# A two-block model kernel: modulation sums re-ordered, head, seams and tail by halves and token tiles

## The chip, the cores and the metric
The kernel runs on one core of a Trainium2 chip. The metric is the device time of one execution in microseconds (us). PE is TensorE (matmuls), PEld its weight loads, DVE VectorE, ACT ScalarE, POOL GpSimd, SP SyncE, whose queue issues most transfers.

## What is computed
One token sequence of 256 tokens and width 2048 goes through two models in fp32. The first block is a norm, an input product (attention of 8 heads and a convolution branch), an output product, a gated residual, and a feed-forward layer of width 8192. The second block has two layers, each with a modulated norm:

```python
shift, scale, gate = m[..., :D_MODEL], m[..., D_MODEL:2 * D_MODEL], m[..., 2 * D_MODEL:]   # m = silu(c) @ mod_w + b
h = _rmsnorm(x, pre_g) * (1 + scale) + shift
proj = h @ w_in
...                                   # even layer: attention over x and ctx; odd layer: pooling
x = x + gate * _rmsnorm(y @ w_out, post_g)
```

The even layer (`ev_`) also modulates a context (`shift_c`, `scale_c`), the odd layer (`od_`) doesn't.

## The kernel before
Every large product is cut into blocks of 512 output columns, each with 8 steps of 256 rows of the weight. A step's weight (128 x 1024 elements on chip) comes by SP's queue into `raw`, 1 MB for two steps. ACT rounds it to `w_hi` (`split_hi`, L530), DVE subtracts to get `w_lo` (`split_lo`, L1053), and PE multiplies activations (`hi`, `lo`) with both. Four slots of `w_hi` and `w_lo` let the splits run four steps ahead: the split of a step can start when PE is through with the step four before it. Blocks follow in this order: `u` (4), `qkv` (6), `out` (4), `ff` (32: four groups of four hidden and four outer blocks), `evq` (4), `evkv` (2, each step double, over x and ctx), `evz` (4, between the attention heads), `evo` (4), `odu` (4), `odg` (4), `pool`, `odo` (4).

Each engine runs its own list of instructions in the written order, and semaphores join them. DVE's list is written by hand: `run_ahead(b, between)` (and `most_ahead`, `each_ahead`) puts two splits and then whatever `between(m)` holds, four times per block: splits (4, 5) and (6, 7) of block b, then (0, 1) and (2, 3) of the next.

In these places stand the modulation sums. Each modulation vector (6 units, L71) is a sum over 16 tiles of 128 rows; each tile comes as two halves of 512 KB into `mod_raw[:, half]` by POOL's queue (`load_half`, L458; `first_loads`, L465), and each half is one multiply-add of 128 x 1024 by DVE into `mod_sum` (`mod_step`, L1080). A unit of two vectors has two such operations per half. POOL issues the load for half n when half n - 2, which used the same buffer, is summed. `each(unit, h0, counts)` (L1103) deals halves out to the four places of a block. When a unit is complete, `mod_turn` turns it by four DVE operations (two block transposes, two reduces), `sum_mod` (L1914) adds the partitions on PE, and `mod_out` writes the columns.

A seam stands between `out` and `ff`, `ff` and `evq`, `evo` and `odu`: ACT squares the last output block of each of the two token tiles, DVE multiplies with the gain (`gained`, `ff_gained`), `post_scale` makes the residual's scale, `gained_products` and `residual_sums` get the next norm without reading the residual again, `add_to_residual` updates X, and `transposes` on PE (L1894, or L1892 at the first) feeds `norm_product`. At the head the same transposes wait for x, the constants and the first norm. At the tail `post_scale` and `add_to_residual` are followed by four output transfers of 512 KB from SP.

POOL's list also copies queries for the second model's heads (`stage_q`), and `head_slots` on POOL puts one load of a modulation half behind each copy.

Of the kernel before, what the change touches and what calls it, by code (L numbers as in the profile page):

```python
# [70 lines left out]
MOD_UNITS = [("ev_gate", 1), ("od_shift", 1), ("ev_shift", 2), ("ev_scale", 2), ("od_scale", 1), ("od_gate", 1)]  # L71
# [30 lines left out]
def build_program(nc, io, out):  # L102
# [6 lines left out]
    with ExitStack() as ctx:  # L109
# [142 lines left out]
        x_first = [sem(f"x_first{i}") for i in range(TT)]  # L252
# [70 lines left out]
        mod_scales = sem("mod_scales")  # L323
# [19 lines left out]
        def _(sp):  # L343
# [24 lines left out]
            sp.dma_start(quad[:], io["quad"]).then_inc(const_in, 16)  # L368
            sp.dma_start(qk_gain[:, 0, :], io["q_norm"].partition_broadcast(P)).then_inc(const_in, 16)
            sp.dma_start(qk_gain[:, 1, :], io["k_norm"].partition_broadcast(P)).then_inc(const_in, 16)  # L370
            sp.dma_start(table[:, 0:512], io["dist_neg"]).then_inc(table_in, 16)

            W = weights["w_in"]
            with sp.Fori(0, 2) as i:
                for par, c0 in ((0, 4096), (1, 3072)):
                    load_block(BLOCK["u"] + 2 * i + par, W, rows(), bass.ds(c0 + BW * i, BW))
# [70 lines left out]
            for n in range(2 * TT):  # L447
                tt, half = n % TT, slice(D // 2 * (n // TT), D // 2 * (n // TT + 1))
                sp.wait_ge(h_ready, 24 + 4 * (n // TT) + TT + tt + 1)
                sp.dma_start(out[tt * P:(tt + 1) * P, half], X[:, tt, half]).then_inc(out_done, 16)  # L450
            sp.wait_ge(out_done, 16 * 2 * TT)
# [3 lines left out]
        def _(pool):  # L455
# [38 lines left out]
            first_loads("od_scale", "od", 1, "ev_scale")  # L494
            load_mod("od_scale", "od", 1, 1, KT // 2 - 1)
# [6 lines left out]
            def head_slots(i, slots, loads=True):  # L502
                for j in slots:
# [4 lines left out]
                    if loads:  # L508
                        load_half("od_scale", "od", 1, KT // 2 + 1 + 2 * i + j // 2, j % 2)
# [531 lines left out]
        def _(dve):  # L1041
# [637 lines left out]
            def evo_beside(n):  # L1679
# [3 lines left out]
                def go(m):  # L1683
# [10 lines left out]
                    if n:  # L1694
                        gate(m)
# [555 lines left out]
```

## Time and profile before
| | us |
|---|---|
| median of 3 runs (range) | 1888.36 (1885.23 to 1890.24) |
| profiled execution, own time | 1888.55 |
| its span, first to last instruction | 1886.9 |
| PE busy in the span | 1820.1 (96%) |
| DVE busy | 1457.7 (77%) |
| ACT busy | 900.3 (48%) |
| mean granted clock of PE | 0.990 |
| read from HBM | 421.23 MB |

The page gives shares over the whole span. The stages have different limits, so the places where PE stands still are to be looked up in windows and in the timelines of the engines around them.

### The profile page before, as it was taken

Reading aid. Unit: us, or ns where it says so; the run is one execution under the profiler, and the core shown is the slowest. Engines: PE = TensorE matmul, PEld = TensorE weight load, DVE = VectorE, ACT = ScalarE, POOL = GpSimd, SP = SyncE. Lnnn points to the kernel's source line nnn. Section 1 sums busy time; section 2 is a strip of 40 time slices with the busy share of each in tenths; the row PEclk is TensorE's granted clock in tenths of the full one; section 3 lists DMA queues with packets and bytes.
Section 4 is the critical chain, followed back from the end, with each engine's and each line's share of the span. In section 5 each row is a group of like instructions: output and inputs, shape, how many; then the busy total and the mean of one; then the engine's idle time right before and its main releaser. Section 6 shows DMA issues by size and latency. Waiting matters only on the chain.

```text
span 1886.9 us, 26488 instructions
## 1 busy us (share of the span) xinstructions
PE 1820.1 (96%) x10068; PEld 1573.7 (83%) x10068; DVE 1457.7 (77%) x1671; ACT 900.3 (48%) x1158; POOL 116.1 (6%) x217
## 2 busy tenths in 40 slices
PE   6999999999999999999999979999999998999997
PEld 6999978788888888888888768888888887888986
DVE  4799996778878898898788987745677677887854
ACT  5343456464434543443344447523556545445452
POOL 0100000100110000000000000000111000000000
PEclk9999999999999999999999989999999999999999
DMA  7865545948998788777977747645544684768662
GB/s 263 291 195 183 159 155 194 331 156 278 325 318 279 240 287 281 234 243 260 266 244 250 262 157 266 200 158 177 168 145 158 242 291 140 252 223 260 209 223 89
DMA packets 189737, 426.94 MB, mean 226 GB/s; under 512 B 12352, under 2 KB 12736, under 8 KB 187840
## 3 DMA queue, kind: packets, MB, share of 16 engines
q1 hardware_dynamic: 161984, 324.80, 50.7%
q0 software_dynamic: 27648, 100.68, 16.3%
q8 instruction: 74, 1.21, 0.3%
q14 instruction: 31, 0.25, 0.0%
HBM read 421.23 MB, written 4.21 MB: 225 GB/s over the span
## 4 chain that ended last, share of the span: by engine, by line
PE 81%; DVE 11%; DMA 4%; ACT 2%; issue 2%; SPq 0%; DVEq 0%; POOLq 0%; ACTq 0%; POOL 0%
PE banks L1831 18%; PE banks L1854 12%; PE banks L1855 12%; PE banks L1856 12%; PE banks L1833 9%; PE banks L1819 4%; PE banks L1820 4%; PE banks L1821 4%; DVE w_lo L1053 3%; DMA mod_raw<-in_ev_mod_w 2%; DVE mod_sum L1242 2%; PE banks L1894 2%; DVE mod_sum L1092 2%; PE banks L2120 1%; PE banks L2136 1%
## 5 line engine op out<-in xcount | busy, mean ns | idle before, releaser
L530 ACT ACTIVATE w_hi<-raw 128x1024 fp32r<-128x1024 f32 x552 | 579.2, 1058 | 697.9 <-PE banks L1856 330.9
L1053 DVE TENSOR_TENSOR w_lo<-raw,w_hi 128x1024 fp32r<-128x1024 f32 x552 | 666.8, 1221 | 233.5 <-ACT w_hi L530 231.4
L1831 PE MATMUL banks<-a_pair,w_hi 128*128 128x512 f32 x1536 | 546.1, 400 | 1.8 <-DVE w_lo L1053 1.5
L1833 PE MATMUL banks<-a_pair,w_lo 128*128 128x256 f32 x1536 | 431.9, 281 | 0.0
L1831 PEld LDWEIGHTS banks<-a_pair,w_hi 128*128 128x128 f32 x1536 | 289.3, 188 | 74.3 <-DVE w_lo L1053 2.2
L1092 DVE SCALAR_TENSOR_TENSOR mod_sum<-mod_raw,silu_c,mod_sum 128x1024 f32<-128x1024 f32 x240 | 301.5, 1280 | 48.0 <-DMA mod_raw<-in_ev_mod_w 24.0
L1854 PE MATMUL banks<-w_hi,b_hi 128*128 128x512 f32 x832 | 326.2, 392 | 4.2 <-DVE w_lo L1053 4.2
L1856 PE MATMUL banks<-w_hi,b_lo 128*128 128x512 f32 x832 | 323.9, 389 | 0.0
L1855 PE MATMUL banks<-w_lo,b_hi 128*128 128x512 f32 x832 | 323.7, 389 | 0.0
L1833 PEld LDWEIGHTS banks<-a_pair,w_lo 128*128 128x128 f32 x1536 | 290.9, 189 | 0.1
L1819 PE MATMUL banks<-a_pair,w_hi 128*128 128x256 f32 x768 | 222.1, 289 | 3.3 <-DVE w_lo L1053 2.9
L1821 PE MATMUL banks<-a_pair,w_lo 128*128 128x256 f32 x768 | 217.9, 284 | 0.0
L1820 PE MATMUL banks<-a_pair,w_hi 128*128 128x256 f32 x768 | 217.9, 284 | 0.0
L1854 PEld LDWEIGHTS banks<-w_hi,b_hi 128*128 128x128 f32 x832 | 156.2, 188 | 39.2 <-issue 7.1
L1856 PEld LDWEIGHTS banks<-w_hi,b_lo 128*128 128x128 f32 x832 | 156.2, 188 | 32.8
L1855 PEld LDWEIGHTS banks<-w_lo,b_hi 128*128 128x128 f32 x832 | 156.2, 188 | 31.9
L1819 PEld LDWEIGHTS banks<-a_pair,w_hi 128*128 128x128 f32 x768 | 148.0, 193 | 4.6 <-DVE w_lo L1053 3.3
L1854 PE MATMUL banks<-w_hi,a_pair 128*128 128x512 f32 x384 | 151.6, 395 | 0.0
L1855 PE MATMUL banks<-w_lo,a_pair 128*128 128x512 f32 x384 | 149.6, 389 | 0.0
L1856 PE MATMUL banks<-w_hi,a_pair 128*128 128x512 f32 x384 | 149.5, 389 | 0.0
L1820 PEld LDWEIGHTS banks<-a_pair,w_hi 128*128 128x128 f32 x768 | 148.1, 193 | 0.1
L1821 PEld LDWEIGHTS banks<-a_pair,w_lo 128*128 128x128 f32 x768 | 147.9, 193 | 0.0
(202 smaller groups left out, 1612.3 us busy)
## 6 DMA issues: line engine op xcount, KB each, us to landing
raw<-in_w_ff SPq DMA_DIRECT2D x128, 1024.0 KB, 6.7
mod_raw<-in_ev_mod_w POOLq DMA_DIRECT2D x96, 512.0 KB, 5.2
mod_raw<-in_od_mod_w POOLq DMA_DIRECT2D x96, 512.0 KB, 5.4
raw<-in_w_in SPq DMA_DIRECT2D x40, 1024.0 KB, 5.1
raw<-in_ev_w_in SPq DMA_DIRECT2D x40, 1024.0 KB, 5.8
raw<-in_od_w_in SPq DMA_DIRECT2D x32, 1024.0 KB, 6.7
raw<-in_w_out SPq DMA_DIRECT2D x16, 1024.0 KB, 5.3
raw<-in_ev_w_out SPq DMA_DIRECT2D x16, 1024.0 KB, 6.9
```

Of the source, the lines that this page charges most:

```text
L530: nc.scalar.activation(w_hi[:, s % SLOTS], raw[:, s // 2, KPS * (s % 2):KPS * (s % 2) + KPS, :], ACT.Copy).then_inc(hi_ready, 1)
L1053: nc.vector.tensor_tensor(w_lo[:, s % SLOTS], raw[:, s // 2, KPS * (s % 2):KPS * (s % 2) + KPS, :], w_hi[:, s % SLOTS].bitcast(F32), ALU.s ...
L1092: nc.vector.scalar_tensor_tensor(s, mod_raw[:, half, :], c, s, ALU.mult, ALU.add).then_inc(mod_acc, 1)
L1242: e = nc.vector.scalar_tensor_tensor(y, src, w, y, ALU.mult, ALU.add)
L1819: nc.tensor.matmul(o, wh, hi[:, k, :], start=first and t == 0 and f % 2 == 0, stop=False, skip_group_check=True)
L1820: nc.tensor.matmul(o, wh, lo[:, k, :], start=False, stop=False, skip_group_check=True)
L1821: last = nc.tensor.matmul(o, wl, hi[:, k, :], start=False, stop=t == KPS - 1, skip_group_check=True)
L1831: nc.tensor.matmul(out[:, f, :], wh, rows[:, :, k, :], start=s == 0 and t == 0, stop=False, skip_group_check=True)
L1833: last = nc.tensor.matmul(out[:, f, T:2 * T], wl, rows[:, 0, k, :], start=False, stop=s == STEPS - 1 and t == KPS - 1, skip_group_check=True)
L1854: nc.tensor.matmul(o, ah, w_hi[:, slot, t, :], start=s == 0 and t == 0, stop=False, skip_group_check=True)
L1855: nc.tensor.matmul(o, ah, w_lo[:, slot, t, :], start=False, stop=False, skip_group_check=True)
L1856: last = nc.tensor.matmul(o, lo[:, k, P * tt:P * (tt + 1)], w_hi[:, slot, t, :], skip_group_check=True, start=False, stop=s == STEPS - 1 a ...
```

## The change
It has these parts.

Head: `ident` is loaded first on a semaphore of its own, x comes in four loads, `cols` behind it, and the other constants behind the first block's weights. ACT squares half a tile and a quarter, DVE squares the last quarter. Norm pairs and weight splits alternate in block one. POOL's first modulation loads wait until four splits are done.

Modulation: the order of units is `ev_gate`, `ev_shift`, `ev_scale`, `od_shift`, `od_scale`, `od_gate`. `od_shift` leaves the `ff` stage and takes the places of `evq` block 2 and `evkv`; `od_scale` takes 24 halves in the heads and 8 in `evo`; `od_gate` has 2 in `evo` and 30 in `odu` and `odg`. `ev_scale`'s turn is at places 228 to 238 of `ff`, its PE sum ahead of the last outer block.

Last steps: in `out`, the last `ff` block, `evo` and `odo`, PE runs steps 6 and 7 of token tile 0 first and then of tile 1, and squares and gain products of tile 0 start at `tile_done`.

Tail: DVE adds five of eight pieces to the residual, ACT and POOL the other three; each piece is its own output transfer.

```diff
-MOD_UNITS = [("ev_gate", 1), ("od_shift", 1), ("ev_shift", 2), ("ev_scale", 2), ("od_scale", 1), ("od_gate", 1)]
+MOD_UNITS = [("ev_gate", 1), ("ev_shift", 2), ("ev_scale", 2), ("od_shift", 1), ("od_scale", 1), ("od_gate", 1)]
+HEAD_HALVES = ((0,), (1, 2), (3,), (4, 5))
+DVE_PIECES = [(0, 0), (1, 0), (0, 1), (1, 1), (0, 2)]
+POOL_PIECES = [(1, 2), (0, 3), (1, 3)]
...
-            for tt in range(TT):
-                sp.dma_start(X[:, tt, :], io["x"][tt * P:(tt + 1) * P, :]).then_inc(x_first[tt], 16)
-            sp.dma_start(ident[:], io["ident"]).then_inc(const_in, 16)
-            sp.dma_start(cols[:], io["cols"]).then_inc(const_in, 16)
+            sp.dma_start(ident[:], io["ident"]).then_inc(ident_in, 16)
+            for n in range(2 * TT):
+                half = slice(D // 2 * (n % 2), D // 2 * (n % 2 + 1))
+                sp.dma_start(X[:, n // 2, half], io["x"][n // 2 * P:(n // 2 + 1) * P, half]).then_inc(x_first[n], 16)
+            sp.dma_start(cols[:], io["cols"]).then_inc(cols_in, 16)
...
+            pool.wait_ge(split_done, 8 + 4)
             first_loads("ev_gate", "ev", 2)
             load_mod("ev_gate", "ev", 2, 1, KT)
-            first_loads("od_shift", "od", 0)
-            load_mod("od_shift", "od", 0, 1, KT)
             first_loads("ev_shift", "ev", 0)
             load_mod("ev_shift", "ev", 0, 1, KT)
             first_loads("ev_scale", "ev", 1)
             load_mod("ev_scale", "ev", 1, 1, KT)
-            first_loads("od_scale", "od", 1, "ev_scale")
-            load_mod("od_scale", "od", 1, 1, KT // 2 - 1)
+            first_loads("od_shift", "od", 0, "ev_scale")
+            load_mod("od_shift", "od", 0, 1, 12)
...
             pool.wait_ge(q_T_ready, 5)
             stage_q(0, 0)
-            load_mod("od_scale", "od", 1, KT // 2 - 1, KT // 2 + 1)
+            load_mod("od_shift", "od", 0, 12, KT)
+            first_loads("od_scale", "od", 1, "od_shift")
             with pool.Fori(0, 3) as i:
                 head_slots(i, range(4))
...
                     else:
-                        halves("od_scale", i, 1)
+                        halves("od_shift", i, 1)
...
-            run_ahead(BLOCK["evkv"], each("od_scale", 4, (1, 2, 1, 2)))
+            run_ahead(BLOCK["evkv"], each("od_shift", 4, (3, 4, 4, 3)))
...
-            run_ahead(BLOCK["evkv"] + 1, each("od_scale", 10, (1, 2, 1, 2)))
+            def last_keys_beside(m):
+                each("od_shift", 18, (4, 4, 4, 2))(m)
+                if m == 3:
+                    mod_turn("od_shift", 0, 0, 3, raw_temp)
+            run_ahead(BLOCK["evkv"] + 1, last_keys_beside)
...
-                    mod_step("od_scale", KT // 2 + 2 * i + j // 2, j % 2)
+                    for c in HEAD_HALVES[j]:
+                        mod_step("od_scale", 3 * i + c // 2, c % 2)
...
+                    if n < 2:
+                        halves("od_scale", 24 + 4 * n + m, 1)
+                    elif n == 2:
+                        turn_parts("od_scale", 0, 1, 3, raw_temp, m, 1)
...
-            gate_steps = [(1, 1, 1, 0)] * 2 + [(1, 0, 1, 0)] * 2 + [(0, 0, 0, 0)] + [(1, 1, 1, 1)] * 2 + [(2, 2, 0, 0)]
+            gate_steps = [(1, 1, 1, 1), (1, 1, 1, 0), (1, 1, 1, 0), (1, 0, 1, 0), (0, 0, 0, 0), (2, 2, 2, 1), (2, 2, 2, 1), (2, 2, 0, 0)]
...
+            def last_steps(steps, a2, hi, lo):
+                for tt in range(TT):
+                    for s, slot in steps:
+                        for t in range(KPS):
...
+                        if tt == TT - 1:
+                            e.then_inc(step_done, 1)
+                    if tt < TT - 1:
+                        e.then_inc(tile_done, 1)
...
-                if n == 1:
-                    sum_mod("od_scale", 1, 3)
+                if n == 2:
+                    sum_mod("od_scale", 2, 3)
```

In each seam the list of DVE changes alike; at `evo` it is:

```diff
-            post_scale(6, lambda: gained_products(NBLK - 1))
+            def last_tile(tt):
+                gained(2 * (2 * NBLK - 1), NBLK - 1, acc[0], gained_tile, [tt])
+                dve.wait_ge(gained_tile, TT * (2 * NBLK - 1) + tt + 1)
+                gained_products(NBLK - 1, [tt])
+            last_tile(0)
+            dve.wait_ge(y_squared, 2 * TT * NBLK)
+            post_scale(6, lambda: last_tile(1))
```

## Rows read from the trace of the kernel before

**Rows 1.** The page, parts 1 and 5: busy shares; VectorE's weight splits.
```profile
PE 1820.1 (96%) x10068; PEld 1573.7 (83%) x10068; DVE 1457.7 (77%) x1671; ACT 900.3 (48%) x1158; POOL 116.1 (6%) x217
...
L1053 DVE TENSOR_TENSOR w_lo<-raw,w_hi 128x1024 fp32r<-128x1024 f32 x552 | 666.8, 1221 | 233.5 <-ACT w_hi L530 231.4
```

**Rows 2.** Timeline, head: start us, us, engine line op, idle before and releaser.
```profile
9.73 1.91 ACT L547 ACTIVATE scratch<-scratch 128x2048 f32<-128x2048 f32 x1 [1.92 <-DMA scratch<-in_x]
...
13.98 0.17 DVE L1212 TENSOR_SCALAR neg_sink<-cols 128x8 f32<-128x8 f32 x1 [13.98 <-DMA qk_gain<-in_k_norm]
...
15.32 6.68 PE L1894 MATMUL banks<-ln_rstd,scratch 128*128 128x128 f32 x32 [15.32 <-DVE ln_rstd L1150]
```

**Rows 3.** Timeline, block one: modulation issues on POOL, and PE's hole.
```profile
62.63 0.53 POOL L461 DMA_DIRECT2D mod_raw<-in_ev_mod_w  x1 [1.56 <-DVE mod_sum L1092]
...
69.78 0.53 POOL L461 DMA_DIRECT2D mod_raw<-in_ev_mod_w  x1 [0.72 <-DVE mod_sum L1092]
...
86.27 0.58 PE L1819 MATMUL banks<-a_pair,w_hi 128*128 128x256 f32 x1 [2.69 <-DVE w_lo L1053]
```

**Rows 4.** Timeline, seam 1 (out to ff).
```profile
376.05 0.60 ACT L736 ACTIVATE scratch<-banks 128x512 bf16<-128x512 f32 x1 [4.38 <-PE banks L1856]
...
380.47 2.82 PE L1892 MATMUL banks<-ident,scratch 128*128 128x128 f32 x12 [4.46 <-DVE scratch L1377]
```

**Rows 5.** Timeline, seam 2 (ff to evq).
```profile
1107.39 1.27 DVE L1528 TENSOR_TENSOR scratch<-scratch,banks 128x512 f32<-128x512 f32 x2
...
1111.57 0.16 DVE L1145 RECIPROCAL resid_s<-norm_s 128x2 f32<-128x2 f32 x1
...
1115.32 6.27 PE L1894 MATMUL banks<-ln_rstd,scratch 128*128 128x128 f32 x32 [7.47 <-DVE ln_rstd L1150]
```

**Rows 6.** Timeline, seam 3 (evo to odu).
```profile
1571.50 5.20 PE L1894 MATMUL banks<-ln_rstd,scratch 128*128 128x128 f32 x32 [7.49 <-DVE ln_rstd L1150]
```

**Rows 7.** Windows: length, busy of PE, PEld, DVE, ACT, POOL, clock, DMA, GB/s.
```profile
4.00:5.00 1.00, 0.00 (x0) 0.00 (x0) 0.00 (x0) 0.00 (x0) 0.00 (x0) 1.00 1.03 426
...
380.50:386.70 6.20, 6.02 (x22) 5.17 (x23) 5.45 (x10) 5.24 (x16) 0.00 (x0) 0.51 0.04 16
...
1036.00:1084.00 48.00, 44.62 (x192) 35.27 (x191) 44.42 (x49) 22.54 (x34) 3.17 (x6) 1.00 0.78 272
```

**Rows 8.** Timeline, odu and odg: a late half, a split of w_hi.
```profile
1613.03 1.28 DVE L1092 SCALAR_TENSOR_TENSOR mod_sum<-mod_raw,silu_c,mod_sum 128x1024 f32<-128x1024 f32 x1 [5.55 <-DMA mod_raw<-in_od_mod_w]
...
1717.95 1.06 ACT L530 ACTIVATE w_hi<-raw 128x1024 fp32r<-128x1024 f32 x1 [1.77 <-PE banks L1833]
```

**Rows 9.** Timeline, tail: residual adds and output transfers.
```profile
1877.78 5.39 DVE L1377 SCALAR_TENSOR_TENSOR scratch<-scratch,resid_s 128x512 f32<-128x512 f32 x8
...
1879.88 3.64 SPq L450 DMA_DIRECT2D out<-scratch  x4
```

**Rows 10.** Timeline, POOL at the first head: an issue and a copy.
```profile
1316.46 0.53 POOL L461 DMA_DIRECT2D mod_raw<-in_od_mod_w  x1 [0.65 <-DVE mod_sum L1092]
...
1317.32 0.62 POOL L507 COPY scratch<-scratch 128x512 f32 x1
```

**Rows 11.** Timeline: end of evo block 2 on ACT; a reduce of a turn.
```profile
1542.29 1.06 ACT L530 ACTIVATE w_hi<-raw 128x1024 fp32r<-128x1024 f32 x1 [1.66 <-PE banks L1856]
...
1762.67 1.22 DVE L1121 TENSOR_REDUCE mod_part<-mod_raw 128x32 f32<-128x1024 f32 x1
```

**Rows 12.** Timeline, evkv and first head: w_hi, first half, the head's maximum.
```profile
1233.17 1.06 ACT L530 ACTIVATE w_hi<-raw 128x1024 fp32r<-128x1024 f32 x1 [4.38 <-PE banks L1856]
...
1235.40 1.28 DVE L1092 SCALAR_TENSOR_TENSOR mod_sum<-mod_raw,silu_c,mod_sum 128x1024 f32<-128x1024 f32 x1
...
1315.74 1.22 DVE L1646 TENSOR_REDUCE soft<-banks 128x2 f32<-128x1024 f32 x1
```

**Rows 13.** mod_raw by tile: landings in 1230:1312 (evkv), in 1330:1470 (heads).
```profile
DMA to landing us min/median/max: 4.7/5.5/6.0
...
DMA to landing us min/median/max: 3.9/4.1/6.1
```

More of the change, by code:

```diff
@@ L446, in _ @@
                 load_block(BLOCK["odo"] + i, W, rows(), bass.ds(BW * i, BW))
[L447 to L451, printed above, removed]
+            for n, (tt, c) in enumerate(DVE_PIECES):
+                part = slice(BW * c, BW * (c + 1))
+                sp.wait_ge(h_ready, 3 * TT * NBLK + n + 1)
+                sp.dma_start(out[tt * P:(tt + 1) * P, part], X[:, tt, part]).then_inc(out_done, 16)
+            sp.wait_ge(out_done, 16 * TT * NBLK)
         @block.gpsimd
@@ L776, in ff_hidden, with gained_squares @@
                     nc.scalar.activation(b_hi[:, 4 * bi:4 * bi + FT, :], relu, ACT.Square).then_inc(hid_hi, 1)
-            def gained_squares(before, i):
-                for tt in range(TT):
+            def gained_squares(before, i, tiles=range(TT)):
+                for tt in tiles:
                     act.wait_ge(gained_tile, TT * (NBLK * before + i) + tt + 1)
@@ L1035, in _ @@
                     split_hi(b + 1, range(4))
-                row_block("odo", n, n % 2)
+                row_block("odo", n, n % 2, range(TT), 4 if n == 3 else 0)
             root(8)
+            act.wait_ge(resid_ready, 1)
+            act.wait_ge(acc_free, 2 + ACC["odo"] + 4)
+            for tt, c in POOL_PIECES:
+                part = slice(BW * c, BW * (c + 1))
+                nc.scalar.activation(Y[:, tt, part], Y[:, tt, part], ACT.Copy, scale=resid_s[:, tt:tt + 1]).then_inc(tail_scaled, 1)
+            for n, (tt, c) in enumerate(POOL_PIECES):
+                part = slice(BW * c, BW * (c + 1))
+                act.wait_ge(tail_ready, n + 1)
+                nc.scalar.dma_start(out[tt * P:(tt + 1) * P, part], X[:, tt, part]).then_inc(out_done, 16)
         @block.vector
@@ L1355, in gained @@
                         e.then_inc(each_tile, 1)
-                if not each_tile:
+                if not each_tile and TT - 1 in tiles:
                     e.then_inc(acc_free, 1)
@@ L1521, in ff_outer, with last_add @@
                     ff_add(g, bi)
-            def last_add(n):
-                block_done(BLOCK["ff"] + 28 + n)
-                for tt in range(TT):
+            def last_add(n, tiles=range(TT)):
+                for tt in tiles:
+                    if n == NBLK - 1 and tt == 0:
+                        dve.wait_ge(tile_done, 2)
+                    else:
+                        block_done(BLOCK["ff"] + 28 + n)
                     part = ff_sum[:, tt, BW * n:BW * (n + 1)]
@@ L1763, in beside @@
                         gate_sum(n - 5)
-                    each("od_gate", 10 + sum(sum(c) for c in gate_steps[:n]), gate_steps[n])(m)
+                    each("od_gate", 2 + sum(sum(c) for c in gate_steps[:n]), gate_steps[n])(m)
                     if n == 7 and m == 2:
@@ L1800, in _ @@
                     dve.wait_ge(grow_in, 64)
-                gained(2 * (2 * NBLK + n), n, acc[n % 2])
-            dve.wait_ge(acc_free, 2 + ACC["odo"] + 4)
-            post_scale(8)
-            add_to_residual()
+                gained(2 * (2 * NBLK + n), n, acc[n % 2], None, range(TT if n < NBLK - 1 else 1))
+            dve.wait_ge(y_squared, 3 * TT * NBLK)
+            post_scale(8, lambda: gained(2 * (3 * NBLK - 1), NBLK - 1, acc[1], None, [1]))
+            dve.sem_inc(resid_ready, 1)
+            for tt, c in DVE_PIECES:
+                part = slice(BW * c, BW * (c + 1))
+                nc.vector.scalar_tensor_tensor(X[:, tt, part], Y[:, tt, part], resid_s[:, tt:tt + 1], X[:, tt, part],
+                                               ALU.mult, ALU.add).then_inc(h_ready, 1)
         @block.tensor
```

285 lines of the change are left out of this document (165 added, 120 removed).

## The prediction

> **What bounds the kernel now.** I read the page's busy shares, then windows of 4 us to find where TensorE (PE) is not full, then the timeline of every engine around each hole. PE is busy for 1820.1 of 1886.9 us [rows 1]: the holes add up to 67 us, and only what shortens or lengthens one, or changes PE's clock, moves the time. They are 15.3 us at the head [rows 2]; 2.7 at 86 [rows 3]; 4.5, 10.1 and 7.5 at the three seams, where a residual sum and a norm stand between two products [rows 4 to 6]; 3.4 in 1036 to 1084 (48.00 less 44.62) [rows 7]; 1.5 near 1613, where VectorE (DVE) waits 5.55 for a modulation load [rows 8]; 12 after the last matmul [rows 9]. DVE is busy 77%, and makes w_lo of each weight step (1.22) in order with all else [rows 1]: whatever it waits for, w_lo waits for too.
>
> **The change, part by part: gains.**
> - Head. DVE's first instruction waits for the last of five constant loads until 13.98; PE starts at 15.32, 1.34 later. The second tile of x was there at 9.73 [rows 2], though 1 MB of modulation weights came beside it. After, ident and x come alone: 2.16 MB at 426 GB/s [rows 7] from about 2.7 us on (first bytes as before) ends at 7.8, landed about 8.1. One 512-column square (0.75 with its read), a reduce (0.3) and the same 1.34 follow: PE at about 10.4. Gain 4.9; bounds 4.2 (x lands 0.7 later) and 5.5. Weights queue behind x and cols alone and are there before the first transposes end; in block one DVE needs 2.1 us per pair and split, PE 3.8 per step with its transposes. The modulation loads start at about 20 us, their first use is at 40: hidden. The hole at 86 stays, as the rounds that make it stay.
> - Seam 1. PE ends at T = 376.0 and goes on at 380.47 [rows 4]. Tile 0's square and product now lie under tile 1's last 12 matmuls (2.7 us), tile 1's product beside the root. What is left from T: square 0.75, reduce and mean 0.4, product 0.65, reciprocal 0.2, two adds 1.4, hand-overs 0.1: T+3.5. Gain 1.0. The two last steps wait for the later one's split; it was ready 1.4 before the earlier one starts, so this adds nothing.
> - Seam 2. PE ends at T = 1104.9, by windows of 1 us. DVE, still turning the scale vectors, comes to the last sum at 1107.39, PE goes on 7.93 later [rows 5]: 10.4. After, the turn is at places 228 to 238 and DVE is free. Tile 0's four operations with hand-overs take 3.0 from T-2.65; then tile 1: sum to T+1.05, square to 1.85, reduce and mean to 2.25, two products to 3.65, and the chain from the reciprocal on as before, 3.75 less a wait of 0.4 [rows 5]: T+7.1. Gain 3.4 (a wait of 0.1 rounded).
> - Seam 3. PE idles 7.49 [rows 6]. After: square 0.75, reduce and mean 0.4, two products 1.5, the same 3.4 behind: T+6.1. Gain 1.4.
> - Hidden layers. od_shift's 32 halves (128x1024) leave them, the two-vector units get 98 places instead of 80, and the turn comes before the last blocks. The 3.4 in 1036 to 1084 come with DVE busy 44.42 of 48 [rows 7]. They go. Gain 3.4, bound below 2.
> - Tail. A square and a product leave the chain, as at seam 1: the first add is 0.9 earlier than 1877.78. Output starts at 1879.88 after three adds of 0.67 [rows 9], now after one: 2.3 earlier; 2 MB then flow at about 400 GB/s if pieces come in time. DVE makes one per 0.67, the queue needs 0.65. No row has an add on GpSimd; its 128x512 copy takes 0.62 [rows 10], so three adds take between 1.9 and, at twice that, 3.8 us, and either way end before the other five pieces are out. Gain 2.3. The Trainium skill, "GPSIMD Engine Reference", section 3.1, measures 4497 ns for a 2048-element add; the estimate from it is 1.1 per piece, and no row here shows it.
>
> Gains: 4.9+1.0+3.4+1.4+3.4+2.3 = 16.4.
>
> **Costs.** A half of a modulation vector is a 512 KB load into one of two buffers, one DVE operation of 1.28, then the next load of that buffer. In block one a buffer's issues are 7.15 apart (62.63, 69.78), so two halves cost 7.1 where PE takes two w_lo in 5.8, and PE runs dry at 86.27 [rows 3].
> - evkv, the largest. 12 halves become 28 (3,4,4,3 and 4,4,4,2 between pairs of splits), with four turn operations behind them (1.22 for a reduce [rows 11], 4.75 in all, bounds 4.5 and 5). PE wants a w_lo per 5.44 (1.06+4.38) [rows 12]. A round is 1.24 (a half behind another) + 0.68 from its end to the issue (0.65 idle and a step of the queue [rows 10]) + the landing: median 5.5 here, where each load meets a 1 MB weight load, 4.1 in the heads, where few do [rows 13]. I take 4.85, near the middle, as of two loads in a place one will meet the weights: round 6.8. I followed it half by half from 1235.4 [rows 12]: a half starts when its buffer has landed and DVE is free, a split 1.1 after PE frees its slot. Splits and halves of the four places of block 0 end at 1235.4/1243.4, 1246.3/1256.9, 1259.3/1270.5, 1272.9/1281.4; head norm and rope take 6.45; block 1: 1290.2/1299.5, 1301.9/1313.0, 1315.4/1326.5, 1328.9/1333.3; the turn 1338.1. The same account with the counts of before gives 1315.8, and DVE came to the first head's maximum at 1315.74 [rows 12]. So it comes 22.3 late. Queued behind it: the maxima, late rope, softmax and the next w_lo. PE stops: its next scores need a query that GpSimd copies only after two loads that wait for this turn, and its transposes need the softmax. Its slack there was nil (it idled 1.4 in four places). Bounds: landing 4.1 gives 14.1, landing 5.2 (the round of block one) 26.2.
> - After such a hole PE comes back at half clock: after seam 1 it was 0.51 over 6.2 us [rows 7]. Half of about 4 us is 2.0 (bounds 0 and 3).
> - evo. PE's sum of the two od vectors stands behind block 2, but the last turn operation stands behind a split whose slot comes free at the block's end T: ACT 1.06 from T [rows 11], split 1.2, reduce 1.2: PE waits 3.5 (bounds 3.3, and 5.2 with the clock lost).
> - odu. Four halves instead of three stand before splits in the place where the third already waits until 1613.03 [rows 8]: 1.2 more.
> - odg. 12 halves become 18 (2,2,2,1 twice, then 2,2). PE takes a w_lo per 2.83 (1.06+1.77) [rows 8], 5.65 for two, against 6.8 for a pair of halves. A split's slack before its PE step is 6.2. By the same account second splits end 5.8 before their step in the first place, 2.6, 0.3 and 0.1 before it in the fifth, eighth and tenth, and 2.6 after it in the last; with the firsts PE loses 4.3. Bounds 0 (landing 4.1) and 7.1 (5.2).
> - Heads: 24 halves instead of 16, 1.3 each in a period of 10.1 where a softmax is ready 4.7 before PE asks: covered; if not, 1.
>
> Costs: 22.3+2.0+3.5+1.2+4.3 = 33.3; net +16.9 on the profiled execution's 1888.55 (span 1886.9 and 1.65 around it), which is 0.2 from the median of the runs shown, 1888.36. Forecast 1905.
>
> **Rivals.**
> 1. Loads come round faster, and the kernel is not slower. At a landing of 3.2 the account gives 6.3 for evkv and 0 for odg: costs 13.0 against 16.4, 1885. It decides from a landing below about 3.6. For it: evkv has light traffic, and od_shift's loads mostly run alone. Against: the shortest landing of the rows is 3.9 [rows 13]. The Trainium skill, "DMA: Bandwidth & Descriptors", section "Anatomy of one DMA", has 2.0 us plus bytes by 436 GB/s, an estimate of 3.2 for 512 KB; by it this rival is the outcome, and the trace's 4.1 and 5.5 speak against it. Chance 0.13.
> 2. DVE's lateness isn't PE's, as I have a queue's order wrong; 3.5+1.2 remain: 1877. Against: the waits stand in the program order of DVE and GpSimd. Chance 0.07.
> 3. All landings near 4.1: costs 14.1+2.0+3.5+1.2 = 20.8, 1893. Chance 0.15.
> 4. The token tiles bring nothing (tile 0's operations hold DVE when tile 1 is ready, or PE's wait for both splits eats it): gains less 5.8, 1911. Chance 0.1.
> 5. The forecast, landings 4.5 to 5.5: 0.55, 1898 to 1914.
>
> **How the numbers follow.** Low end: rival 3 and a seam 1 whose clock holds (-3), 1889. High end: landing 5.2 and clocks lost, 1888.5-16.4+26.2+3+5.2+1.2+7.1 = 1915, with half of rival 4's loss 1919. A measurement tells 0.3%, 5.7 us, from no change, so "same" is 1882.7 to 1894. Faster: rival 2 and part of rival 1, 0.12. Same: the rest of rival 1 and half of rival 3, 0.15. Slower 0.73.
>
> **What would show it.** PE's first matmul near 10.4; seam holes of 3.5, 7.1 and 6.1; none in 1036 to 1084; a hole of some 20 at the first head, with many DVE waits on od modulation loads before it; one of 3.5 behind evo block 2; several of 1 to 1.5 in odg. I am wrong if evkv's landings are near 3.5, or if PE goes on while DVE lags.

## The result, and the profile after

| | before | after |
|---|---|---|
| median of the runs, us | 1887.09 (4 runs, 1885.23 to 1890.24) | 1921.59 (4 runs, 1918.45 to 1926.26) |
| ratio | | 1.0183, 95% interval 1.0156 to 1.021 |
| profiled span, us | 1886.9 | 1921.2 |
| TensorE (PE) busy, us | 1820.1 | 1829.4 |
| VectorE (DVE) busy, us | 1457.7 | 1462.4 |

The change costs 34 us; 17 were forecast, and 1921.6 lies 2.6 above the top of the range. The first view to read is the page's busy shares with the modulation line, of the kernel after; it answers [rows 1].

```profile
PE 1829.4 (95%) x10068; PEld 1581.5 (82%) x10068; DVE 1462.4 (76%) x1673; ACT 903.6 (47%) x1165; POOL 121.3 (6%) x220
...
L1127 DVE SCALAR_TENSOR_TENSOR mod_sum<-mod_raw,silu_c,mod_sum 128x1024 f32<-128x1024 f32 x240 | 301.1, 1280 | 88.9 <-DMA mod_raw<-in_od_mod_w 65.5
```

PE is idle 25 us more (1921.2 less 1829.4 is 91.8; it was 66.8) and busy 9 us longer for the same 10068 matmuls, which is time at the lower clock. The modulation operations waited 88.9 us in all, 65.5 of it for od loads. The waits of PE, kernel after (line waited for, us in total, times, longest):

```profile
PE banks L1981 <- DVE ln_rstd L1185: 24.7, 3, 12.0
PE banks L2234 <- POOL scratch L507: 20.8, 1, 20.8
PE banks L1897 <- DVE w_lo L1088: 5.7, 5, 2.9
PE banks L1885 <- DVE w_lo L1088: 5.4, 4, 3.2
PE banks L2010 <- issue: 3.6, 1, 3.6
...
PE banks L1885 <- DVE scratch L1815: 3.4, 1, 3.4
PE banks L1979 <- DVE scratch L1414: 3.3, 1, 3.3
PE banks L2169 <- DVE scratch L1628: 3.0, 1, 3.0
```

L1981 is the head (12.0, was 15.3) with seams 2 and 3; L1979 is seam 1 (3.3, was 4.5 in [rows 4]). L2234 is the first head, L2169 the key transposes in evkv, L2010 the sum in evo, L1897 the small holes of odu and odg, and the L1885 that waits for scratch the one before the pooling product. The L1885 that waits for w_lo is mostly block one (3.6 of its 5.4; the 3.2 is the hole that was 2.69 in [rows 3]). The hole at the first head is made by a timeline of DVE like this one (evkv's second block):

```profile
1281.04 2.47 DVE L1127 SCALAR_TENSOR_TENSOR mod_sum<-mod_raw,silu_c,mod_sum 128x1024 f32<-128x1024 f32 x2
1287.66 2.52 DVE L1127 SCALAR_TENSOR_TENSOR mod_sum<-mod_raw,silu_c,mod_sum 128x1024 f32<-128x1024 f32 x2 [4.15 <-DMA mod_raw<-in_od_mod_w]
1290.11 2.75 DVE L1088 TENSOR_TENSOR w_lo<-raw,w_hi 128x1024 fp32r<-128x1024 f32 x2
...
1317.45 2.35 DVE L1088 TENSOR_TENSOR w_lo<-raw,w_hi 128x1024 fp32r<-128x1024 f32 x2
...
1328.26 1.22 DVE L1156 TENSOR_REDUCE mod_part<-mod_raw 128x32 f32<-128x1024 f32 x1
1329.40 1.22 DVE L1696 TENSOR_REDUCE soft<-banks 128x2 f32<-128x1024 f32 x1
```

One sees two halves, 4.15 us of nothing, two halves, and only then the next two w_lo. The first head's maximum comes at 1329.40. PE had ended its last product before that and waited from 1311.

Where the 34 us are. Windows of 2 us over both traces give PE's idle time, and, as busy time multiplied by (1 less the granted clock), at most what the lower clock cost:

| stretch of the trace, us | idle, after less before | clock, after less before | the steps of the prediction there |
|---|---|---|---|
| head (first matmul 11.98, was 15.32) | -3.3 | | -4.9 |
| 14 to 372, without the head | +0.8 | +3.1 | 0 |
| 372 to 392, seam 1 | -1.1 | -1.3 | -1.0 |
| 392 to 1084, hidden layers | -3.4 | 0 | -3.4 |
| 1084 to 1120, seam 2 | -3.4 | -0.7 | -3.4 |
| 1120 to 1350, evkv and first head | +23.3 | +1.7 | +24.3 |
| 1350 to 1540, other heads | 0 | 0 | 0 |
| 1540 to 1600, evo and seam 3 | +2.1 | +4.0 | +2.1 |
| 1600 to 1740, odu and odg | +1.3 | +1.7 | +1.2 |
| 1740 to 1860, rest of odg, pool | +6.2 | +3.3 | +4.3 |
| tail (last matmul to end 14.7, was 12.0) | +2.7 | | -2.3 |

The sum is 36.9 for 34.3 in the spans. Most of the difference lies between seams 1 and 2: PE goes on behind seam 2 at 1103.78, 11.5 earlier than the 1115.32 of [rows 5], where the rows down to there give 8.7. Neither column shows what the rest is.

### The profile page after: what moved, and what is told of

Same layout as the page of the kernel before. It is cut to its first block and busy times, and to the rows that moved or that the text cites. A ratio compares the mean times of both kernels' runs of the same rounds, so it can differ in the third digit from the quotient of the medians.

```text
span 1921.2 us, 26445 instructions
## 1 busy us (share of the span) xinstructions
PE 1829.4 (95%) x10068; PEld 1581.5 (82%) x10068; DVE 1462.4 (76%) x1673; ACT 903.6 (47%) x1165; POOL 121.3 (6%) x220
## 5 line engine op out<-in xcount | busy, mean ns | idle before, releaser
L1897 PE MATMUL banks<-a_pair,w_hi 128*128 128x512 f32 x1536 | 546.3, 400 | 5.9 <-DVE w_lo L1088 5.7
L1127 DVE SCALAR_TENSOR_TENSOR mod_sum<-mod_raw,silu_c,mod_sum 128x1024 f32<-128x1024 f32 x240 | 301.1, 1280 | 88.9 <-DMA mod_raw<-in_od_mod_w 65.5
L1897 PEld LDWEIGHTS banks<-a_pair,w_hi 128*128 128x128 f32 x1536 | 290.2, 189 | 78.5 <-DVE w_lo L1088 7.4
L1920 PE MATMUL banks<-w_hi,b_hi 128*128 128x512 f32 x808 | 317.4, 393 | 0.8 <-DVE w_lo L1088 0.8
L1922 PE MATMUL banks<-w_hi,b_lo 128*128 128x512 f32 x808 | 315.4, 390 | 0.0
L1921 PE MATMUL banks<-w_lo,b_hi 128*128 128x512 f32 x808 | 315.4, 390 | 0.0
L1885 PE MATMUL banks<-a_pair,w_hi 128*128 128x256 f32 x768 | 222.7, 290 | 4.4 <-DVE w_lo L1088 4.4
L1922 PEld LDWEIGHTS banks<-w_hi,b_lo 128*128 128x128 f32 x808 | 152.3, 188 | 31.9
L1921 PEld LDWEIGHTS banks<-w_lo,b_hi 128*128 128x128 f32 x808 | 152.3, 188 | 31.5
L1885 PEld LDWEIGHTS banks<-a_pair,w_hi 128*128 128x128 f32 x768 | 148.6, 193 | 5.8 <-DVE w_lo L1088 4.0
L1920 PE MATMUL banks<-w_hi,a_pair 128*128 128x512 f32 x376 | 148.7, 395 | 0.2 <-DVE w_lo L1088 0.2
L1922 PE MATMUL banks<-w_hi,a_pair 128*128 128x512 f32 x376 | 146.4, 389 | 0.0
```

What stands on the lines that cost most here:

```text
L1127: nc.vector.scalar_tensor_tensor(s, mod_raw[:, half, :], c, s, ALU.mult, ALU.add).then_inc(mod_acc, 1)
L1885: nc.tensor.matmul(o, wh, hi[:, k, :], start=first and t == 0 and f % 2 == 0, stop=False, skip_group_check=True)
L1897: nc.tensor.matmul(out[:, f, :], wh, rows[:, :, k, :], start=s == 0 and t == 0, stop=False, skip_group_check=True)
L1920: nc.tensor.matmul(o, ah, w_hi[:, slot, t, :], start=s == 0 and t == 0, stop=False, skip_group_check=True)
L1921: nc.tensor.matmul(o, ah, w_lo[:, slot, t, :], start=False, stop=False, skip_group_check=True)
L1922: last = nc.tensor.matmul(o, lo[:, k, P * tt:P * (tt + 1)], w_hi[:, slot, t, :], skip_group_check=True, start=False, stop=s == STEPS - 1 a ...
```

## Experiments

Fourteen kernels; "before" was run beside each. Three of them (GpSimd's adds alone, x in whole rows, no hold) have one profiled execution each, so that only their traces are read. The question of the first four: what carries the loss, and does a half of a modulation vector cost DVE's work or the round of its load?

**The order of the vectors.** MOD_UNITS, the counts and the sums go back; head, token tiles and tail stay.

```diff
-MOD_UNITS = [("ev_gate", 1), ("ev_shift", 2), ("ev_scale", 2), ("od_shift", 1), ...
+MOD_UNITS = [("ev_gate", 1), ("od_shift", 1), ("ev_shift", 2), ("ev_scale", 2), ...
-each("od_shift", 4, (3, 4, 4, 3))
+each("od_scale", 4, (1, 2, 1, 2))
```

> The changed kernel with the modulation vectors in the order and at the places of the kernel before; head, last steps by token tile and tail stay as changed. Theory (the reorder carries the loss): the hole of 20.8 us at the first head, the 3.6 behind evo's block 2 and the 7 us of odg's holes go, the 10 us hole at seam 2 comes back save about 1; head, seams 1 and 3 and the tail sum to about 0 by the two traces (seam 1 goes on 0.5 earlier, seam 3 1.5 less, tail 2.7 more): 1887 us, within 3. Rival (head, tiles or tail carry it): above 1900.

1882.58 us, ratio 0.9976 (0.9964 to 0.9988). So the reorder alone costs 39 us, and the rest of the change is a gain of 5, though this kernel still has the long tail.

**No loads.** `load_mod("od_shift", ...)` is cut after the first two pairs, and DVE doesn't wait for the others.

```diff
-            load_mod("od_shift", "od", 0, 1, 12)
+            load_mod("od_shift", "od", 0, 1, 2)
-            load_mod("od_shift", "od", 0, 12, KT)
```

> The changed kernel without the loads of the last 28 halves of od_shift (those of evkv and its neighbours): VectorE still does every one of the 28 operations, on what the buffers last held, so od_shift is not computed. Theory (a half costs a round of operation, issue and landing, 6.8 us per two): the work alone, two w_lo and 3.5 halves, is 6.8 us in PE's 10.9 per place, so VectorE keeps step, and only the turn (4.8 us) and the last halves stand before the first head: its hole falls from 20.8 to 3 to 7 us, the time to about 1902 to 1906. Rival (the 16 more operations of 1.24 us, 20 us of VectorE's work, are the cause): hole and time stay within 5 us of what they are, 1917 or more.

1898.28, ratio 1.0059 (1.0039 to 1.0079): 23 us less than the changed kernel with the same work on DVE. The wait at the first head:

```profile
PE banks L2239 <- POOL scratch L507: 4.0, 1, 4.0
```

The 3.0 at the key transposes went too. In DVE's list the turn (4.75) is what stands in front of the first head, and 4.0 stay; no run has this kernel without the turn. The rival, 20 us of work, is out. The time is below the theory's 1902. Of the 22.1 between the two spans, 20.3 are idle time from 1120 to 1350 and 2.3 the tail (12.4 for 14.7, see below); evo's hole stays at 3.6, and odu and odg took 3.3 back (13.4 idle, where the changed kernel has 10.1).

**Half the bytes.** The loads of od_shift and od_gate move 512 columns instead of 1024.

```diff
-                nc.gpsimd.dma_start(mod_raw[:, half, :],
+                n = MH // 2 if unit in ("od_shift", "od_gate") else MH
+                nc.gpsimd.dma_start(mod_raw[:, half, 0:n],
```

> The changed kernel with every od_shift and od_gate load after the first two cut to half its columns (256 KB instead of 512); VectorE's operations stay whole, so the two vectors are not computed right. Theory (a landing is mostly waiting beside the weights' loads and a fixed part): the median landing in evkv falls from 4.7 to 3.7 to 4.1, a round of two from about 6.8 to 6.0, the hole at the first head from 20.8 to 8 to 13, and odg's small holes go: 1904 to 1911. Rival (the fixed part is 2.0 and the rest goes by bytes): landings of 2.6 and a hole near the 4.0 that no loads left: 1895 to 1898.

1895.44, ratio 1.0038 (1.0025 to 1.0051). The time that an od load takes from issue to landing, minimum, median, maximum between 1225 and 1335 us, of the changed kernel and of this one, and this one's wait at the first head:

```profile
DMA to landing us min/median/max: 3.8/4.7/6.8
```

```profile
DMA to landing us min/median/max: 2.8/3.5/7.3
...
PE banks L2235 <- POOL scratch L508: 12.2, 1, 12.2
```

Landing (3.5) and hole (12.2) came out nearer to the theory's numbers than to the rival's 2.6 and 4.0; the time is the rival's, since odu and odg, which the theory put at little, gave more: between 1600 and 1860 the idle time fell from 10.1 to 1.4. Two sizes give a line, as an estimate: 256 KB more cost 1.2 us, 218 GB/s, and 2.3 us are left at no bytes. The rule weighed in the prediction (the Trainium skill, "DMA: Bandwidth & Descriptors", section "Anatomy of one DMA", 2.0 us plus bytes by 436 GB/s) has the fixed part nearly right and the bytes at twice the speed of this estimate. What slows them, the weights' loads or something else, no run here separates.

**The queue of GpSimd.** The copies for PE go ahead of the two loads that wait for the turn.

```diff
             load_mod("od_shift", "od", 0, 12, KT)
+            stage_q(1, 1)
+            pool.wait_ge(pv_done, HEAD2 + 2)
+            nc.gpsimd.tensor_copy(v_stage2, ...)
             first_loads("od_scale", "od", 1, "od_shift")
```

> The changed kernel with GpSimd's copies of the second query and of the first values ahead of the two od_scale loads that wait for od_shift's turn. Theory (VectorE's own lateness, not GpSimd's queue, holds the first head): PE computes the second scores early and then waits for the first head's softmax, which VectorE reaches at 1329.4 as now; the hole changes its name and is 0 to 2 us shorter, the time 1919.5 to 1921.5. Rival (the copy stuck behind the loads is what PE lacks): a hole of 20.8 falls below 5, the time to about 1905.

1923.21, ratio 1.0191 (1.0173 to 1.0209): no gain; the rival is out, and the time lies above the theory's 1921.5, within the noise of the changed kernel (1918.45 to 1926.26). The hole is cut in two, 10.9 before the transposes of the first head's softmax and 8.5 before the next copy:

```profile
PE banks L2214 <- DVE mod_sum L1719: 10.9, 1, 10.9
PE banks L2239 <- POOL scratch L507: 8.5, 1, 8.5
```

The first line is DVE's own lateness. Together the two are 1.4 shorter than 20.8, and the lower clock between 1120 and 1350 took up to 5.8 in this trace, 2.0 in that of the changed kernel. The page's name for a hole (POOL, in the changed kernel) was only the last in the row.

**The turn in evo.** The four turn operations stand behind the first three pairs of w_lo of block 2, two, one, one and none; the text below names the counts once wrongly and once, at its end, rightly.

```diff
-                        turn_parts("od_scale", 0, 1, 3, raw_temp, m, 1)
+                        turn_parts("od_scale", 0, 1, 3, raw_temp, (0, 2, 3, 4)[m], (2, 1, 1, 0)[m])
```

> The changed kernel with od_scale's four turn operations one, two, one, none behind the four pairs of w_lo of evo's block 2 (now one each), so that none stands behind the pair whose slots come free at the block's end. With counts two, one, one as built: all four are done at the third. Theory: PE's wait of 3.6 us before the sum of the two vectors goes, with the 1.2 us at lower clock behind it: 3.6 to 5 us less, 1917. Rival (the wait is for PE's own sequence or another operation): the 3.6 stay, 1921.

1916.91, ratio 1.0157 (1.014 to 1.0174): 4.7 less for a hole of 3.6. Windows of PE, first of the changed kernel, then of this one (length, busy of PE, PEld, DVE, ACT, POOL, then clock, DMA share, GB/s):

```profile
1556.00:1560.00 4.00, 1.16 (x18) 1.06 (x19) 3.55 (x4) 2.84 (x9) 0.69 (x2) 0.70 0.50 128
1560.00:1564.00 4.00, 4.00 (x10) 3.09 (x10) 0.00 (x0) 0.00 (x0) 0.36 (x1) 0.50 0.98 326
```

```profile
1556.00:1560.00 4.00, 4.00 (x19) 3.27 (x19) 2.53 (x4) 3.83 (x10) 0.00 (x0) 1.00 0.97 334
1560.00:1564.00 4.00, 4.00 (x19) 3.30 (x18) 2.68 (x5) 1.09 (x2) 0.00 (x0) 1.00 0.71 264
```

Behind the hole PE did 10 matmuls in 4 us at a clock of 0.50 (1.2 GHz), without it 19. In the changed kernel's trace this stretch cost up to 2.8. It doesn't always come: six kernels have the same hole of 3.6 with the same code around it, and the clock behind it cost 2.8, 2.9, 3.0 and 1.5 in the traces of the changed kernel and those with half the bytes, without od_shift's and without od_gate's loads, but nothing in those with the copies moved and with the tail on DVE. Behind the hole of the kernel with the copies moved, which ends at 1561.08:

```profile
1560.00:1564.00 4.00, 2.92 (x28) 2.44 (x29) 2.17 (x3) 1.11 (x4) 1.05 (x2) 1.00 0.70 219
1564.00:1568.00 4.00, 4.00 (x19) 3.34 (x18) 1.23 (x1) 1.93 (x2) 0.00 (x0) 1.00 0.86 300
```

So of the 4.7 between the medians 3.6 are the hole; the 1.1 on top is no more than the spread of the executions.

**odu and odg.** od_gate's loads are left out after the first two.

> The changed kernel without od_gate's loads after the first two; VectorE does all its 32 operations, so od_gate is not computed right. Theory (in odu and odg too the round of a load, not the work, makes w_lo late): the hole of 2.9 us at 1632 stays within 1 (its halves are od_gate's, so it should fall to 1.5 or less), the seven holes of odg (7.0 us in all) fall below 1.5, and the stretches at half clock behind them (some 5 us) go with them: 8 to 13 us less, 1909 to 1914. Rival (18 operations of 1.24 us are too many for the place): 3.4 us before the first pooling product and most of the others stay, 1918 or more.

1901.03, ratio 1.0072 (1.0053 to 1.0091): 20.6 less than the changed kernel, far more than 8 to 13. Windows, the changed kernel first:

```profile
1600.00:1640.00 40.00, 37.10 (x214) 32.46 (x213) 28.34 (x31) 17.51 (x23) 2.12 (x4) 0.96 0.58 191
1740.00:1770.00 30.00, 28.01 (x149) 23.82 (x148) 20.98 (x18) 12.96 (x13) 4.24 (x8) 0.94 0.84 286
1770.00:1800.00 30.00, 24.98 (x154) 21.61 (x152) 25.35 (x22) 11.52 (x11) 2.12 (x4) 1.00 0.72 248
```

```profile
1600.00:1640.00 40.00, 40.00 (x238) 35.45 (x237) 33.87 (x33) 17.78 (x20) 0.00 (x0) 1.00 0.60 196
1740.00:1770.00 30.00, 30.00 (x175) 26.47 (x174) 26.22 (x23) 14.00 (x14) 0.00 (x0) 1.00 0.54 177
1770.00:1800.00 30.00, 30.00 (x234) 28.78 (x233) 25.90 (x35) 14.34 (x15) 0.00 (x0) 1.00 0.57 176
```

All holes from 1600 on are gone, 10.1 us, and the lower clock with them, 5.0: 15 of the 20.6. Another 2.5 are the tail, 12.2 from the last matmul to the end instead of 14.7, though its adds are the same. The rest isn't settled. In this profiled execution (1896.5, the fastest of four) block one had no clock loss at all (0.0, against 4.7 in that of the changed kernel), which is chance, since nothing there differs. The holes' share of the clock is firmer here than in evo: five traces with these holes lost 3.0 to 5.5 from 1600 to 1860, and this one and that with half the bytes, which have almost none, lost 0.0.

**The tail.** All eight pieces of the last add on DVE.

```diff
-                nc.gpsimd.tensor_tensor(X[:, tt, part], Y[:, tt, part], X[:, tt, part], ALU.add).then_inc(tail_ready, 1)
-                nc.scalar.activation(Y[:, tt, part], Y[:, tt, part], ACT.Copy, scale=resid_s[:, tt:tt + 1])...
-            for tt, c in DVE_PIECES:
+            for _, (tt, c) in PIECES:
```

> The changed kernel with all eight 128x512 pieces of the last residual add on VectorE; they leave on the same two queues. Theory (GpSimd and VectorE slow each other: five adds of 1.29 us mean and three of 1.71 beside each other, against 0.67 alone): each add takes 0.67 again, the last ends 7.8 us after the last matmul instead of 8.4, the output ends 9.6 to 10.1 after it, and the time is 0.3 to 1 us shorter, up to 4 if the 4.5 us between the last output packet and the end go back to the 0.9 of the kernel before. Rival (no sharing: the adds are slow by something else in the tail, the output queues or the lower clock): VectorE's adds stay above 1 us, and eight of them end 3 us later than now.

1918.02, ratio 1.0163 (1.0126 to 1.02), executions from 1911.2 to 1921.5, too wide to say by the medians. The traces do. Kernel after (the second fence line is the view of one line: minimum, median and maximum duration in ns), then this one:

```profile
1908.48 6.43 DVE L1869 SCALAR_TENSOR_TENSOR scratch<-scratch,resid_s 128x512 f32<-128x512 f32 x5 [0.16 <-DVE resid_s L1180]
L1869 DVE SCALAR_TENSOR_TENSOR scratch<-scratch,resid_s x5: 745/1745/1757, 1908.5 to 1913.2; 128x512 f32<-128x512 f32 x5
1909.22 5.14 POOL L536 TENSOR_TENSOR scratch<-scratch 128x512 f32<-128x512 f32 x3 [125.30 <-ACT scratch L1068]
```

```profile
1903.73 5.39 DVE L1862 SCALAR_TENSOR_TENSOR scratch<-scratch,resid_s 128x512 f32<-128x512 f32 x8
```

An add on DVE takes 0.745 us alone and 1.745 beside one on GpSimd (in a row they overlap a little: eight take 5.39, 0.67 each). From the last matmul to the end it is 11.1 us here, 14.7 in the changed kernel.

**GpSimd's adds alone.** Three of them behind the last piece, into a buffer nobody reads, in the fast version below.

```diff
+            pool.wait_ge(h_ready, 3 * TT * NBLK + 8)
+            for c in range(3):
+                nc.gpsimd.tensor_tensor(Y[:, 0, part], Y[:, 0, part], X[:, 0, part], ALU.add)
```

> The faster version (all eight pieces on VectorE) with three 128x512 adds on GpSimd behind the last piece, into a buffer that nobody reads, so that they run alone. Theory (the 1.7 us of an add and VectorE's 1.75 came from each other): GpSimd's adds take 0.9 to 1.3 us alone, VectorE's stay at 0.67. The 3.4 us between last output packet and end that the kernels with GpSimd's adds had more than those without come back if the adds themselves bring them (a load of instructions at 1918 stood in that gap): end 14 to 15 us after the last matmul. Rival: GpSimd's add is 1.7 alone and only VectorE suffers; end at 11 to 12.

```profile
1875.24 3.69 POOL L535 TENSOR_TENSOR scratch<-scratch 128x512 f32<-128x512 f32 x3 [128.68 <-DVE scratch L1860]
```

1.23 each alone, 1.71 beside DVE: both suffer. The end comes at 1885.8, 6.9 after GpSimd's last add (1878.93) and 17.9 after the last matmul, where the fast version has 11.1. In the changed kernel it also came 6.8 after GpSimd's last add (1914.36 to 1921.2), though its output was out by 1917, while without adds on GpSimd the end came 3.5 to 3.9 after DVE's last add. So with these adds the kernel can end later than its output asks, but the adds alone don't do it. In the kernels without od_shift's and without od_gate's loads the same adds were followed by the end 4.6 and 4.4 later, and that was 4.0 and 3.9 behind DVE's last add, much as in kernels with no add on GpSimd. A load of 0.01 MB on the instruction queue follows the adds in all these traces, with and without the late end, and not in that of the kernel with the tail on DVE; so it doesn't explain the late end either. What the two kernels share is that GpSimd issues 28 and 30 fewer loads. The cause stays open.

**The head alone**, in the kernel before.

> The kernel before with the new head alone (ident and x in halves first, pair and split in turn, modulation loads held until the twelfth w_lo). Theory from the two traces (the first matmul comes 3.3 us earlier, but the hole near 84 is longer and TensorE's clock behind it lower, and a second dip near 272 takes the rest): 1886 to 1888, no gain; seam 1 is reached at 376 as before. Rival (the gain is carried through): 1883.8, seam 1 at 372.7.

1883.96, ratio 0.9981 (0.9968 to 0.9993): the rival's time, 3.6 gained for a first matmul 3.1 earlier; its trace reaches seam 1 at 374.5, between the theory's 376 and the rival's 372.7. The theory read chance as cause. In the changed kernel's trace the gain was nearly gone behind seam 1, where PE goes on at 379.8 (380.5 before), but two kernels with the same code up to there, those with the order of before and with the tail on DVE, go on at 375.9, and that without od_gate's loads at 373.9. The clock behind the small holes at 84 and 272 differs from execution to execution.

**What the head is bound by.** Two kernels, from the fast version: x in whole rows; and no hold on the modulation loads.

```diff
-                sp.dma_start(X[:, n // 2, half], io["x"][..., half]).then_inc(x_first[n], 16)
+                sp.dma_start(X[:, tt, :], io["x"][tt * P:(tt + 1) * P, :]).then_inc(x_first[tt], 16)
```

> The faster version with x as two loads of whole rows, as before, instead of four of half rows; ident stays ahead, the modulation loads stay held. Theory (half rows move slower: 177 to 300 GB/s between 2.4 and 4.2 us of the changed kernel against 410 to 437 in the kernel before): the second tile lands at 8.3 to 8.7 instead of 9.69, TensorE's first matmul comes at 11.3 to 11.7 instead of 11.98. Rival (the rate is set by the start of the chip's loads and not by the rows): 9.7 and 12.8, as whole tiles leave ScalarE's last squares later.

```diff
-            pool.wait_ge(split_done, 8 + 4)
```

> The faster version without GpSimd's wait for the twelfth w_lo: the first modulation loads (1 MB) start beside x, as before. Theory (x and they share 400 GB/s, 1 MB is 2.5 us in all, of which x bears half at most): the last piece of x lands at 10 to 11 instead of 9.69 and the first matmul comes 0.3 to 1.3 later; at 84 the hole stays. Rival (the other queue takes only what x's leaves idle, as with 9.73 in the kernel before): no change, 12.0.

The last of x reaches ScalarE at 9.69 in the changed kernel (9.82 in the fast version); as whole rows it is 9.19, but ScalarE's squares then follow each other and PE starts at 12.52. Without the hold it is 12.53, and PE starts at 14.83:

```profile
11.98 1.41 PE L1981 MATMUL banks<-ln_rstd,scratch 128*128 128x128 f32 x5 [11.98 <-DVE ln_rstd L1185]
```

```profile
14.83 1.40 PE L1969 MATMUL banks<-ln_rstd,scratch 128*128 128x128 f32 x5 [14.83 <-DVE ln_rstd L1175]
```

The hold is most of the head's gain (2.7 of 3.3), more than the 0.3 to 1.3 that were expected: x is later by what 1 MB takes at about 400 GB/s. With whole rows PE's start comes near the rival's, and the landing lies halfway.

**The version that beats both.** Order of before, new head and token tiles, tail on DVE; and the same with ev_scale turned early.

> The modulation vectors in the order of before, the head and the last steps by token tile as changed, and the eight pieces of the last add on VectorE, leaving on two queues. Theory: 3.6 us less than the same kernel with GpSimd's three adds (1882.6 beside a before of 1887.6), as the stretch from the last matmul to the end is 11.1 us instead of 14.7: about 1879, 8 to 9 below before. Rival (the tail's end is set by something else, and the 3.6 were chance): 1882 to 1883.

1877.55, ratio 0.9949 (0.9933 to 0.9966), 9.6 below before.

> As the version before it in this call, and the turn of ev_scale at places 228 to 238 as in the changed kernel, with od_shift's halves in 44 places, ev_shift's in 74 and ev_scale's in 73 (48, 80 and 79 before). Theory: VectorE is free at seam 2, its hole falls from about 10 to 6.7 us; the hole near 1036 to 1084, where VectorE was busy 44.4 of 48 us, spreads over the earlier hidden layers, where 8% more halves per place stand against 5 to 8% of slack, and costs 0 to 2 more: 1876 to 1879. Rival (VectorE is the bound there, 4 to 8 us more in the hidden layers): above 1880.

1878.45, ratio 0.9954 (0.9937 to 0.9971). The hole at seam 2 fell from 11.3 to 6.7 (1084 to 1120 us), and the 3.7 between 1030 and 1084 went as well; what it gained there it lost in w_lo waits elsewhere, and the two can't be told apart.

**Token tiles off**, in the first of these: step by step with both tiles.

```diff
-                for tt in range(TT):
-                    for s, slot in steps:
+                for s, slot in steps:
+                    for tt in range(TT):
```

> The faster version (modulation order of before, new head, eight pieces on VectorE) with TensorE's last two steps in the order of before, step by step with both token tiles in each: tile 0 is then ready one 0.7 us group of matmuls before the end instead of 2.7 us. All else stays. Theory (what stands in tile 0's square and products must lie under matmuls): seam 1's hole grows from 3.3 to about 4.5, seam 3's from 6.1 to about 7.5, the stretch to the first output piece by 0.9, and seam 2, where VectorE is late with the scale vectors anyway, by 0 to 1: 3.3 to 4.3 us more, 1881 to 1882. Rival (token tiles bring nothing): 1877.5, holes as they are.

1881.02, ratio 0.9974 (0.9961 to 0.9987), 3.5 above by the medians, as forecast; but the intervals of the two ratios meet (0.9961 and 0.9966), and the traces show only 0.7 of it: seam 3 idles 6.8 instead of 6.1, seams 1 and 2 are unchanged (3.5; 11.2 and 11.3), and the two spans are 1878.4 and 1878.6. So of seam 1's gain nothing hangs on PE's order. What is left of the change there is that each tile is waited for by itself; no run takes that alone away. Where the rest of the medians' 3.5 lies, if it is more than noise, stays open.

## Why the prediction was wrong

The direction, the place and the mechanism were right, the size was half. Step by step:

- **evkv and first head: right.** Forecast 22.3 plus 2.0 for the clock, found 23.3 idle and 1.7 clock. The account holds place by place but for one: against the schedule of before, the changed kernel is 12.5 earlier at evkv's start, and with that added block 0's first three places are within 0.8 of it, the fourth ends at 1284.9 for 1281.4, and block 1's places end at 1302.7, 1316.3, 1330.0, 1336.9 and the turn at 1341.9, where 1299.5, 1313.0, 1326.5, 1333.3 and 1338.1 stood, 3.2 to 3.8 late. The landing taken, 4.85, was 4.7. One wait of PE within it was missing: the key transposes behind the head norm, 3.0, so that the first head's hole itself is 20.8. DVE came to the first head's maximum 26.2 late, not 22.3, and PE idled only 1.0 more than forecast, so that the size is in part luck. That the round and not the work is the cause is shown by the kernel without loads and the one with half the bytes.
- **The clock: the step that failed first.** It was costed once, 2.0 at the first head, and put at nothing behind the new holes of evo, odu and odg. In the changed kernel's trace those stretches lost +4.0 in evo and seam 3 and +5.0 in odu and odg, at most, which is about 9 of the 17 us missed. The second is borne out by the others (3.0 to 5.5 with the holes, 0.0 without). The first is in part luck of the execution: behind evo's hole six traces lost between 0.0 and 3.0. The bound for evo, "5.2 with the clock lost", stood in the text, and the lower value was taken. Another 3.1 of the trace's loss, in block one, is chance.
- **The tail: failed, 5.0.** Forecast -2.3, found +2.7. The sum took DVE's add at 0.67 and GpSimd's at 0.6 to 1.3, each as if alone. The first output is issued at 1909.26, 2.7 after the last matmul (5.0 before), as forecast; then the adds slowed each other, and the end came late. The trace shows the slowing by the two durations of one line, 745 and 1745 ns; the mechanism is in the Trainium skill, "SBUF — State Buffer", section "SBUF: two separate sides": the two engines take turns on one port pair for whole instructions when VectorE reads two operands from SBUF. By it a pair of adds costs 0.67 + 1.1, an estimate that takes 1.1 from the Trainium skill's "GPSIMD Engine Reference", section 3.1; 1.71 was measured. The five adds on DVE take 6.4 us beside GpSimd's three where all eight on DVE take 5.4, and the last ends 8.4 behind the last matmul instead of 7.2. That is 1.2 of the 5.0 missed; 2.4 are the late end, whose cause is open. The last 1.4 have nothing to do with GpSimd: with all adds on DVE the stretch is 11.1, which is 0.9 less than before and not 2.3. The first output leaves as early as forecast (2.6 behind the last matmul), but from there to the end it takes 8.5 in eight pieces on two queues, and 7.0 in the four transfers of before. I had weighed the price of GpSimd's add and neither its neighbour nor the output in pieces.
- **Head: mechanism right, size off by 1.6.** x landed at 9.69 instead of 8.1, as it came at 142 to 328 GB/s from 2 to 5 us (windows of 1 us), not at 426. The rest of the chain took 2.29 for 2.4. With the hold gone, x is 2.7 later: the step "x comes alone" was right.
- **odg: right cause, 2 short.** The halves cost 6.2 instead of 4.3 by idle time. The last hole, before the pooling product, is 3.4 where 1.0 stood before: 2.4 more, and the account had 2.6. The miss is in the places before it, 3.8 for 1.7, and 1.8 of that is one hole at 1764.
- **Seams 1 to 3 and hidden layers: right.** 3.5, 6.7 and 6.1 idle against T+3.5, 7.1 and 6.1; no hole from 1026 to 1084. Rival 4 (token tiles bring nothing) holds for PE's order at seams 1 and 2, where the holes stay as they are without it; at seam 3 the order is worth 0.7.
- **evo's sum: right**, 3.6 for 3.5, and the turn moved in evo takes it away.
- **Rival 1** (short landings) and **rival 2** (lateness is not PE's) are out, by 4.7 in the changed kernel and by the copies moved ahead.

The range was built from the landings; the clock and a tail that gets longer had little or no room in it. Its high end adds up to 1917.7 by its own terms, not 1919. Without the tail's 5.0, or without the 5.0 of the clock in odu and odg, the time would have been about 1916.6, so neither alone put it outside.

## What to carry to other kernels

Work put beside a full engine costs the round of its buffer, not its own time: operation, issue and landing by the number of buffers. Compare that with the period between the steps it stands among before moving it. Give each new hole on TensorE a range for the stretch at 1.2 GHz behind it, from nothing to what the holes of the traces show (here up to 3.0 for one of 3.6), and put the high value into the high end. And before giving a second engine part of a short job, ask what it shares with the first, and look at what comes after its last operation.

## What the runs showed of the hardware

- 128x512 adds with both operands in SBUF: VectorE 0.67 in a row (0.745 the first), 1.745 beside one on GpSimd; GpSimd 1.23 alone, 1.71 beside VectorE.
- With adds on GpSimd at the end, the kernel ended 6.8 to 6.9 us behind the last of them in most traces and 4.4 and 4.6 in two, where GpSimd had issued fewer loads; without them it ended 3.5 to 3.9 us behind VectorE's last add. Why is open.
- A load from GpSimd's queue beside the weights' took 4.7 us for 512 KB and 3.5 for 256 KB (medians of 1225 to 1335 us).
- The same code up to seam 1 lost between 0.0 and 4.7 us to the lower clock behind the same small holes, from execution to execution; one profiled execution doesn't tell a gain of 3 us there. Behind the same hole of 3.6 us in evo six traces lost 0.0, 0.0, 1.5, 2.8, 2.9 and 3.0.
